# Meta tokens' probabilities of four heads in one zero-padded tile, and 528 keys as 264 + 264, in a hybrid attention block

## What is computed

```python
logits = einsum('bqhd,bkd->bqhk', qb, k) * d_head ** -0.5
logits = where(valid, logits, NEG)
probs = softmax(logits, axis=-1)
out = einsum('bqhk,bkd->bqhd', probs, v)
```

## Time and profile before

| | us |
|---|---|
| median of 3 runs | 1407.05 (1406.35 to 1408.79) |
| the profiled execution | 1405.66 |
| its span | 1403.9 |

### The profile page before, as it was taken

How to read it: one execution, slowest core, us unless ns; L and a number is a source line. 1 busy time by engine, 2 the same in 40 slices (tenths; PEclk the granted TensorE clock), 3 DMA queues, 4 the chain that set the end, 5 groups by cost and what they waited for, 6 DMA issues and landing times.

```text
span 1403.9 us, 23076 instructions
## 1 busy us (share of the span) xinstructions
PE 1381.5 (98%) x8864; PEld 1234.3 (88%) x8864; DVE 646.1 (46%) x1076; ACT 498.8 (36%) x727; POOL 529.2 (38%) x248
## 2 busy tenths in 40 slices
PE   7999999999999999999999999999999999999998
PEld 7989889799999999999998978887778888888887
DVE  5486878545333333322222889686553333332000
ACT  4354444724222222322233434456332322322222
POOL 3542211024444444444446343101344444444444
PEclk9999999999999999999999999999999999999999
DMA  5212101012222222232323121100122222323234
GB/s 184 71 61 76 47 30 32 31 59 76 92 90 90 90 90 90 90 105 90 105 75 97 55 76 54 37 16 31 60 91 94 100 90 90 102 92 97 98 105 149
DMA packets 32169, 112.46 MB, mean 80 GB/s; under 512 B 3696, under 2 KB 4080, under 8 KB 31984
## 3 DMA queue, kind: packets, MB, share of 16 engines
q1 hardware_dynamic: 31392, 110.59, 23.7%
q10 hardware_dynamic: 720, 1.09, 0.2%
HBM read 109.57 MB, written 2.10 MB: 80 GB/s over the span
## 4 chain that ended last, share of the span: by engine, by line
PE 54%; issue 32%; POOL 8%; DVE 4%; ACT 1%; DMA 0%; POOLq 0%; SPq 0%; DVEq 0%; ACTq 0%
PE ps L859 19%; PE ps L865 9%; POOL wlo L749 8%; PE ps L949 5%; PE ps L950 5%; PE ps L955 5%; PE ps L1069 2%; PE ps L1042 2%; PE ps L1054 1%; PE ps L963 1%; PE ps L1022 1%; PE ps L973 1%; DVE score L1615 1%; PE ps L915 1%; PE ps L1093 1%
## 5 line engine op out<-in xcount | busy, mean ns | idle before, releaser
L749 POOL TENSOR_TENSOR wlo<-raw,whi 128x1024 fp32r<-128x1024 f32 x202 | 498.8, 2470 | 855.5 <-ACT whi L1222 854.9
L1222 ACT ACTIVATE whi<-raw 128x1024 fp32r<-128x1024 f32 x202 | 213.8, 1058 | 595.9 <-PE ps L865 548.8
L859 PE MATMUL ps<-xhi,whi 128*128 128x264 f32 (+1 forms) x1096 | 327.7, 322 | 7.3 <-ACT whi L1222 7.2
L859 PE MATMUL ps<-xlo,whi 128*128 128x264 f32 (+1 forms) x1096 | 326.3, 321 | 0.0
L859 PEld LDWEIGHTS ps<-xhi,whi 128*128 128x128 f32 x1096 | 206.8, 189 | 24.6 <-ACT whi L1222 7.0
L859 PEld LDWEIGHTS ps<-xlo,whi 128*128 128x128 f32 x1096 | 206.6, 188 | 16.0
L865 PE MATMUL ps<-xhi,wlo 128*128 128x264 f32 (+1 forms) x1096 | 195.4, 321 | 0.4 <-POOL wlo L749 0.2
L949 PE MATMUL ps<-xhi,whi 128*128 128x264 f32 (+1 forms) x632 | 180.8, 315 | 0.1
L865 PEld LDWEIGHTS ps<-xhi,wlo 128*128 128x128 f32 x1096 | 162.9, 188 | 17.3 <-issue 1.0
L950 PE MATMUL ps<-xlo,whi 128*128 128x264 f32 (+1 forms) x632 | 171.4, 300 | 0.0
L859 PE MATMUL ps<-hlo,whi 128*128 128x264 f32 (+1 forms) x528 | 157.5, 321 | 0.0
(11 more groups left out here) (169 smaller groups left out, 1728.9 us busy)
## 6 DMA issues: line engine op xcount, KB each, us to landing
raw<-in_weights SPq DMA_DIRECT2D x202, 512.0 KB, 3.4
out_hT<-h SPq DMA_DIRECT2D x8, 256.0 KB, 4.2
h<-in_hT SPq DMA_DIRECT2D x4, 264.0 KB, 6.7
h<-in_hT ACTq DMA_DIRECT2D x4, 264.0 KB, 6.0
cst<-in_consts SPq DMA_DIRECT2D x1, 1046.0 KB, 10.1
par_all<-in_params SPq DMA_DIRECT2D x1, 144.0 KB, 9.7
par_all<-in_params SPq DMA_DIRECT2D x1, 140.0 KB, 9.7
cst<-in_consts SPq DMA_DIRECT2D x1, 128.0 KB, 4.9
```

What stands on the lines that cost most here:

```text
L749: nc.gpsimd.tensor_tensor(wlo[:, b], raw[:, b], whi[:, b].bitcast(F32), ALU.subtract).then_inc(split_done, 1)
L859: nc.tensor.matmul(bank(bank_no, cut.stop - cut.start), whi[:, b, k % KT], x(k)[t][:, cut], start=(first and k == ks[0] and t == 0), stop= ...
L1222: return nc.scalar.activation(whi[:, b], raw[:, b], ACT.Copy).then_inc(hi_done, 1)
```

## The change

Four heads' probabilities of the 16 meta keys go to a tile of their own, `p_meta`, in which head h has columns 32 h to 32 h + 15 and the rest are zeros. When a group's four heads are there, one transpose (`meta_turn`) turns the whole tile, ACT copies it to `p_meta_t`, and one matmul over 128 rows (`meta_values`) multiplies it by `v_meta`, in which head h's meta values stand in rows 32 h to 32 h + 15 and columns 65 h to 65 h + 64, with zeros elsewhere: 260 columns at once, added to what the four heads' values have left in bank 3. The heads' own turn and values begin with j = 1, so block 0 has none. ACT's exponential is made in two parts, the 16 meta keys into `p_meta` and the rest in place. 528 keys are moved in two pieces of 264, which lie around a bank's edge (`keys_at`). A turn takes one bank for every block. The planner's times follow, and `BIAS` has other numbers, so the order of the lists is another.

```diff
-        "turn": [("turn", *h) for h in HEADS[l]],
-        "values": [("values", *h) for h in HEADS[l]],
+        "turn": [("turn", *h) for h in TURNED[l]],
+        "values": [("values", *h) for h in TURNED[l]],
+        "meta_turn": [("meta_turn", *a) for a in ATTENDED[l]],
+        "meta_values": [("meta_values", *a) for a in ATTENDED[l]],
...
-        cut = [min(keys, 512)] + ([keys - 512] if keys > 512 else [])
+        cut = [keys] if keys <= 512 else [keys // 2] * 2
...
-    block = job[1] if job[0] == "index" else job[2] if job[0] in ("logits", "turn") else 0
+    block = job[1] if job[0] == "index" else job[2] if job[0] == "logits" else 0
...
-            probs_t = mb("probs_t", [QB, 2, NQ, QB])
+            probs_t = mb("probs_t", [QB, 2, NQ - 1, QB])
+            p_meta = mb("p_meta", [QB, 2, 4, 32])
+            p_meta_t = mb("p_meta_t", [QB, 2, QB])
...
+        def keys_at(b, n):
+            return b * 512 + (512 - n // 2 if n > 512 else 0)
...
+                    nc.gpsimd.memset(p_meta[:], 0.0).then_inc(ev.masks_ready, 1)
+                    pool.wait_ge(ev.masks_ready, 6)
+                    nc.gpsimd.memset(v_meta[:], 0.0).then_inc(ev.masks_ready, 1)
+                    pool.wait_ge(ev.masks_ready, 7)
+                    for hd in range(4):
+                        nc.gpsimd.memset(v_meta[meta_rows(hd), :, hd, 64:65], 1.0).then_inc(ev.masks_ready, 1)
+                        pool.wait_ge(ev.masks_ready, hd + 8)
...
-                    return [(0, min(n, 512))] + ([(512, n)] if n > 512 else [])
+                    return [(0, n)] if n <= 512 else [(0, n // 2), (n // 2, n)]
...
 def turn(g, i, hd):
-                    for j in range(i + 1):
-                        col = b0 * 512 + j * 128
-                        keys = tokens_of(j) if j or i == 0 else slice(0, QB)
-                        rows = rows_of(i).stop
-                        ins = nc.tensor.transpose(ps[0:keys.stop - keys.start, col:col + rows], probs[0:rows, u % 3, keys],
-                                                  cols(C_ID, rows, slice(0, rows)))
+                    for j in range(1, i + 1):
+                        col = b0 * 512 + (j - 1) * QB
+                        ins = nc.tensor.transpose(ps[:, col:col + QB], probs[:, u % 3, tokens_of(j)], ident)
...
 def values(g, i, hd):
-                    for j in range(i + 1):
-                        keys, queries = rows_of(j), rows_of(i)
-                        v = v_dsa[keys, j] if g == 0 else v_fox[keys, j, hd]
-                        ins = nc.tensor.matmul(ps[queries, 3 * 512 + hd * 65:3 * 512 + (hd + 1) * 65],
-                                               probs_t[keys, u % 2, j, queries], v, start=(j == 0), stop=(j == i))
+                    for j in range(1, i + 1):
+                        v = v_dsa[:, j - 1] if g == 0 else v_fox[:, j - 1, hd]
+                        ins = nc.tensor.matmul(ps[:, 3 * 512 + hd * 65:3 * 512 + (hd + 1) * 65], probs_t[:, t % 2, j - 1], v,
+                                               start=(hd == 0 and j == 1), stop=False)
+                def meta_turn(g, i):
+                    b0, done = job_begin(("meta_turn", g, i))
+                    pe.wait_ge(ev.probs_ready, LOGITS[l][(g, i, 3)] + 1)
+                    rows = rows_of(i).stop
+                    nc.tensor.transpose(bank(b0, rows), p_meta[0:rows, GROUPS[l][(g, i)] % 2].rearrange("p h c -> p (h c)"),
+                                        cols(C_ID, rows, slice(0, rows))).then_inc(done, 1)
+                def meta_values(g, i):
+                    wait_taken(("meta_turn", g, i))
+                    nc.tensor.matmul(ps[rows_of(i), 3 * 512:3 * 512 + 260], p_meta_t[:, GROUPS[l][(g, i)] % 2, rows_of(i)],
+                                     v_meta[:, g].rearrange("p h d -> p (h d)"), start=(i == 0), stop=True).then_inc(ev.group_done, 1)
...
 def turn_tile(k):   (ACT)
+                        for hd in range(4):
+                            nc.scalar.activation(v_meta[meta_rows(hd), 0, hd, 0:64], turned(b0, META)[:, 0, ROW_DV:ROW_DV + 64], ACT.Copy)
...
+                            nc.scalar.activation(v_meta[meta_rows(hd), 1, hd, 0:64], turned(b0, META)[:, 0, hh * 64:(hh + 1) * 64], ACT.Copy)
...
 def logits(g, i, hd):   (ACT)
-                    nc.scalar.activation(p, p, ACT.Exp, bias=stat[rows_of(i), 0, w:w + 1],
-                                         scale=-1.0).then_inc(ev.probs_ready, 1)
+                    if grp >= 2:
+                        wait_done(("meta_turn",) + ATTENDED[l][grp - 2])
+                    ins = nc.scalar.activation(p_meta[rows, grp % 2, hd, 0:META], probs[rows, u % 3, 0:META], ACT.Exp,
+                                               bias=stat[rows, 0, w:w + 1], scale=-1.0)
+                    if i:
+                        p = probs[:, u % 3, META:keys_to(i)]
+                        ins = nc.scalar.activation(p, p, ACT.Exp, bias=stat[:, 0, w:w + 1], scale=-1.0)
+                    ins.then_inc(ev.probs_ready, 1)
...
+                def meta_turn(g, i):   (ACT)
+                    nc.scalar.activation(p_meta_t[:, n % 2, rows], bank(b0, rows.stop), ACT.Copy).then_inc(taken, 1)
...
 def logits(g, i, hd):   (DVE)
-                    if u >= 3:
+                    if u >= 3 and HEADS[l][u - 3][1]:
                         wait_done(("turn",) + HEADS[l][u - 3])
+                    elif u >= 3:
+                        dve.wait_ge(ev.probs_ready, u - 2)
...
-                    dve.wait_ge(ev.values_done, u + 1)
+                    dve.wait_ge(ev.group_done, grp + 1)
```

More of the change, by code:

```diff
@@ L124 @@
 HEADS = [[(g, i, h) for g, i in ATTENDED[l] for h in range(4)] for l in range(DEPTH)]
+TURNED = [[(g, i, h) for g, i, h in HEADS[l] if i] for l in range(DEPTH)]
 NORM_ORDER = [DKIK, DQ, DQ + 1, FQ, FQ + 1, FK, FK + 1] + [GV + h for h in range(4)]
@@ L287, in work @@
         n = ATTENDED[l].index((g, i))
-        return [(PE, 0.225 * (i + 1) if i else 0.12, [(("turn", *a), ACTE)] + [turned(t) for t in ((FV, FV + 1) if g else (SMALL,))] +
+        return [(PE, 0.225 * i, [(("turn", *a), ACTE)] + [turned(t) for t in ((FV, FV + 1) if g else (SMALL,))] +
                  ([(("scale", *ATTENDED[l][n - 1]), DVEE)] if h == 0 and n else []))]
+    if kind == "meta_turn":
+        n = ATTENDED[l].index(a)
+        return [(PE, 0.109, [(("logits", *a, 3), ACTE)]),
+                (ACTE, act_us(QB, True), [(("meta_values", *ATTENDED[l][n - 2]), PE)] if n >= 2 else [])]
+    if kind == "meta_values":
+        g, i = a
+        n = ATTENDED[l].index(a)
+        return [(PE, 0.45, [(("meta_turn", *a), ACTE)] + [turned(t) for t in ((FV, FV + 1) if g else (SMALL,))] +
+                 ([(("scale", *ATTENDED[l][n - 1]), DVEE)] if n else []) + ([(("values", *a, 3), PE)] if i else []))]
     if kind == "scale":
         n = ATTENDED[l].index(a)
-        return [(DVEE, 0.62, [(("values", *a, 3), PE)] + ([(("back", *ATTENDED[l][n - 1]), PE)] if n else []))]
+        return [(DVEE, 0.62, [(("meta_values", *a), PE)] + ([(("back", *ATTENDED[l][n - 1]), PE)] if n else []))]
     if kind == "back":
@@ L322, in work @@
     raise ValueError(kind)
-AUX_KINDS = ("prenorm", "norm", "rope", "turn_tile", "gate", "index", "logits", "turn", "turn_k", "gla_att", "gla_out",
+AUX_KINDS = ("prenorm", "norm", "rope", "turn_tile", "gate", "index", "logits", "turn", "meta_turn", "turn_k", "gla_att", "gla_out",
              "gla_kv", "back")
@@ L513 @@
 GROUPS = [{s: n for n, s in enumerate(groups)} for groups in ATTENDED]
+TURNS = [{s: n for n, s in enumerate(heads)} for heads in TURNED]
 ROPES = {k: n for n, k in enumerate(ROPE_ORDER)}
@@ L1040, in logits @@
                             pe.wait_ge(ev.sums_spread, 4)
+                    at = keys_at(b0, n)
                     for a, z in pieces(n):
-                        ins = nc.tensor.matmul(ps[rows_of(i), b0 * 512 + a:b0 * 512 + z], q, key[:, a:z], start=True, stop=True)
+                        ins = nc.tensor.matmul(ps[rows_of(i), at + a:at + z], q, key[:, a:z], start=True, stop=True)
                     ins.then_inc(done, 1)
@@ L1152, in _ @@
                 do = dict(prenorm=prenorm, proj=proj, norm=norm, rope=rope, turn_tile=turn_tile, turn_k=turn_k, gate=gate,
-                          index=index, logits=logits, turn=turn, values=values, back=back, gla_att=gla_att,
+                          index=index, logits=logits, turn=turn, values=values, meta_turn=meta_turn,
+                          meta_values=meta_values, back=back, gla_att=gla_att,
                           gla_out=gla_out, gla_kv=gla_kv, out=out)
@@ L1420, in _ @@
                           turn_k=turn_k, gate=gate, gate_log=gate_log, gate_exp=gate_exp, fox_log=fox_log,
-                          index=index, logits=logits, turn=turn, mixed=mixed,
+                          index=index, logits=logits, turn=turn, meta_turn=meta_turn, mixed=mixed,
                           gla_out=gla_out, silu=silu, gla_mix=gla_mix)
@@ L1675, in logits @@
```

(2 more changed lines are left out.)

82 lines of the change are left out of this document (50 added, 32 removed).

## The result

The changed kernel takes a median of 1366.67 us (1366.61 to 1366.74 in four runs), the kernel before 1407.92 (1406.35 to 1409.17) beside it: a ratio of 0.971 (0.969 to 0.972), faster by 41 us. The forecast was 1377; the sign and PE's sum came as forecast, the half clock and the give-back did not, and the time lies 1.3 us under the low end of the range. The profiled execution took 1366.64 us with a span of 1364.8, against 1405.66 and 1403.9: the span is 39.1 us shorter.

What follows compares the result with a forecast made beforehand. PE, busy 98%, was taken as the bound. Its terms, -32.0 - 3.3 - 7.0 - 3.8 + 10.6 = -35.5 us, plus 5 given back, made -30 us: 1377 us from 1407.05, range 1368 to 1392.

Steps and rivals of the forecast that it cites:

- the half clock: Mixer stretches below full clock, 5.1 us missing; they could go or come, taken as 0, bounds -7 to +7.
- the give-back: Mixers' ends: a DVE 88% full in layer 1 makes others wait, returning 5 us over both layers.
- The 16-row matmuls (32.0 us): First keys' values on PE: 64 matmuls removed at 0.50 us each by starts, half in each layer.
- Block 0: Layer 0's 16-query block: its 8 heads' values and transposes go, 3.3 us less on PE.
- transposes: The first-key transposes of the other 64 heads go from PE, 0.11 us each, 7.0 us less.
- 264 + 264: 528-key index and logits jobs on PE: equal pieces save 0.16 us for each of 24 heads, 3.8 us.
- ACT: Split exponentials at a net 0.28 us per head and changed copies add about 18 us, hidden beside PE.
- "Order" part: Planner's rearranged lists on every engine: taken as 0, bounds -7 to +7 from waits and half-clock time.
- DVE as the bound: First rival: DVE becomes the limit late in the mixers, giving back half: -18, 1389 us; chance 0.16.
- Further down (waits and half clock gone too): Outcome below the forecast's 1370 to 1383 us, without those losses; chance 0.04.
- the sixteen rows at 0.22: Second rival: each 16-row matmul on PE is worth only 0.22 us: -17.6, 1389 us; chance 0.08.
- ACT uncovered: Third rival: ACT's longer way per head and meta round trips exposed, 44 against 35.5, 1415 us; chance 0.05.

Runs made afterwards that it cites:

- first run: Kernel before, with the first matmul of each of 64 values jobs over 128 rows instead of 16: 1379.80 us against 1408.23, ratio 0.980.
- fourth run: Changed kernel with 528 keys moved as 512 + 16 again, order untouched: 1369.93 us, ratio 0.973 to the kernel before.
- second run: Kernel before with 528 keys moved as two equal pieces of 264, order untouched: 1406.71 us, ratio 0.999.
- sixth run: Changed kernel with every second round of DVE's selection left out: 1366.30 us, ratio 0.972 to the kernel before.
- the seventh: Changed kernel with one more 8-column exponential on ACT for each of 72 heads: 1368.11 us, ratio 0.973 to the kernel before.
- third run: Changed kernel with the planner's old biases, so only the order of the lists differs: 1396.67 us, ratio 0.993 to the kernel before.
- tenth run: Kernel before, with first-key matmuls over 128 rows only in each layer's last two groups (16 heads): 1396.60 us, ratio 0.993.
- eighth run: Changed kernel with the gate's matmuls and block 0's meta turns widened from 16 to 128 rows: 1364.64 us, ratio 0.971 to the kernel before.
- eleventh: Kernel before, with first-key matmuls over 128 rows in all but each layer's last two groups (48 heads): 1392.01 us, ratio 0.989.
- twelfth run: Kernel before, unchanged, profiled once more for the spread of its runs: 1409.12 us, span 1407.3.
- fifth run: Kernel before with first-key matmuls over 128 rows and 528 keys as two pieces of 264: 1379.36 us, ratio 0.981.

## Why the prediction was right and where it was wrong

**The 16-row matmuls (32.0 us): right, and the reading too.** Taking distances between starts instead of durations gave 0.50 where the durations gave 0.22. The first run isolates the part in dispute: 0.30 for the change of rows, forecast 0.28. The Trainium skill, page "TensorEngine Tiling (Array Packing)", section "Tiling Modes", says that changing the tiling mode drains TensorE; it gives no number for it. The first run agrees with a price of that kind, 0.30 us for going to 16 rows and back; that the mechanism is this drain no run here shows. The Trainium skill's sentence on weight loads, which the prediction set against its term, holds in this trace (page "TensorE: Matmul & The Clock Gate", section "LDWEIGHTS (loading the stationary operand)"): in the kernel before the loads last 183 to 190 ns on 16 rows and 190 to 193 on 128. The 304 and 289 ns that the prediction took for it are the matmuls' durations, and neither says what the starts cost.

**Block 0, transposes: right** (values and transposes together -38.6, forecast -36.5). **264 + 264: right in the changed kernel** (3.3 us of 3.8, by the fourth run), and worth little in the kernel before (the second run). A term's price by starts held in both; how much of it reached the end depended on the clock.

**Added work on PE: right**, 10.3 against 10.6 us.

**ACT: right in its sum of durations, too high as cover needed.** The durations rose by 17.4 us (524.9 to 542.3), forecast 18, but the engine's busy time only by 9.1 (498.8 to 507.9), because neighbours overlap. The new exponential in the changed kernel, grouped by line and shape, and one of them in order of time:

```profile
L1435 ACT ACTIVATE p_meta<-probs,stat 128x16 f32<-128x16 f32 x64 | 19.3, 302 | 23.9 <-DVE stat L1752 23.0 <-PE ps L1085 0.7
```

```profile
940.27 0.30 ACT L1435 ACTIVATE p_meta<-probs,stat 128x16 f32<-128x16 f32 x1
940.47 0.39 ACT L1439 ACTIVATE probs<-probs,stat 128x128 f32<-128x128 f32 x1
```

The small exponential lasts 0.30 and puts the next one off by 940.47 - 940.27 = 0.20 (0.205 as the mean of 64). The prediction read PE by starts and ACT by durations; by starts a head's way grew by 0.2, not 0.28.

**The step that failed first: "I give back 5 us for this over both layers".** Its reason was that a DVE 88% full makes others wait. DVE was 87% full, and waits grew by 1.5 us in all. The sixth run takes a twelfth of DVE's work away and gains 0.4; the seventh adds to ACT and loses 1.4. There was hardly anything to give back. What was late next was no engine but the order, and the order that came with the change was fitted to it: with the old biases the give-back would have been 30 us (third run), beyond the bound of +7 in the "Order" part. That bound was drawn from the waits seen before, which say nothing of how well another list fits; the forecast owed its luck to the new biases there.

**The step that failed second: half clock, "I take 0, bounds -7".** The missing clock was read in two stretches of before, 5.1 us; there are three, 6.8. 5.1 of these went. The prediction named both of their likely sources, "a wait of 2.8 us and stretches of short matmuls at the mixers' ends", and left it there. The 16 rows that the change takes out were just those short matmuls: the tenth run shows that they carried the half clock at both ends (5.1 us; the 1.7 in the middle followed the wait, and the changed kernel has as much at 70 to 80 us). With this read, the forecast would have been -35.5 - 5.1 = -40.6 on a span that fell by 39.1. The miss in numbers: -35.5 + 5 = -30.5 was forecast and -39.1 measured; of these 8.6 us 5.1 are the clock and 3.5 the give-back (5 less the 1.5 of waits).

**The range.** Its low end, 1368, was the full -35.5 and 3.5 us of clock. The bound of -7 was kept beside the give-back and never set on top of -35.5: 1407.05 - 35.5 - 7 = 1364.55 would have held the result. "Further down (waits and half clock gone too)" had 0.04; the half clock did go, the waits did not.

**"Both fall alike": not quite.** The median fell by 41.2 us and the profiled executions by 39.0. The execution of before that was profiled misses 6.8 us of clock, where the runs of before miss 7.3 to 8.7 in the mean, and the kernel after has almost none to vary. A gain that removes a cause of spread is larger in the median than in a lucky execution.

**The rivals.** DVE as the bound fell by the sixth run, the sixteen rows at 0.22 by the first, ACT uncovered by the seventh. Rival 1's "9 tenths busy in layer 1's" is the one stretch of 810 to 820 us; over layer 1's mixer DVE had 152.5 of 190 us, 80%. No change was far off. The new order as a rival of its own was missing from the list; it could have decided the sign had the biases not been refitted.

## What to carry to other kernels

Read a full, pipelined engine by its starts, and look ahead of and behind an odd shape: an operation on few rows can cost more than the same one on 128, and padding it with zeros or unused rows may be free. When PE's work changes shape, look at what stands in the stretches at half clock before; if it is the work that goes, the clock may come back with it and belongs in the sum. A saving of a few us can go back to the clock, so read the granted clock of every run before calling a term worth nothing. In a kernel whose lists come from a planner, a change of tiles and a new fit of the order have to be judged together: either alone was worth 11 us or cost 18, both 41.

## What was not expected of the hardware

- A matmul on 16 rows between those on 128 costs 0.30 us more than the same on 128 rows, over 64 such places (first run); a gate job, four instructions on 16 rows with 266 columns, goes from 1.09 to 0.70 us over 128 rows (eighth run).
- Two kernels with the same waits and the same busy shares at a mixer's end (9.33, then 8.98 of 10 us) had a clock of 1.00 and of 0.66 to 0.86 there, by whether the matmuls just before ran on 128 or 16 rows (tenth and eleventh runs).
- The granted clock varies between executions of one kernel: 6.8 and 10.2 us missing, and this alone is the 3.4 us between two spans (twelfth run). Behind one and the same wait of PE (2.8 us in seven profiles) the clock was halved in five and full in two.
- A saving can come back as missing clock: of 3.0 us at full clock some 2 went so (second run), of 3.3 some 2.4 (fifth run).
